# The experts' products as float32 matmuls on four column quarters of TensorE's array, in place of three float32r products on the whole array

## The reference

```python
def moe_swiglu(x, w_router, w_gu, w_down):
    ...
    logits = (t @ w_router).astype(jnp.float32)
    top_v, top_i = lax.top_k(logits, TOP_K)
    top_w = jax.nn.softmax(top_v, axis=-1)
    gates = jnp.sum(jax.nn.one_hot(top_i, N_EXPERTS, dtype=jnp.float32) * top_w[..., None], axis=1)
    out = jnp.zeros_like(t)
    for e in range(N_EXPERTS):
        out = out + gates[:, e:e + 1].astype(t.dtype) * swiglu(t, w_gu[e], w_down[e])
```

## Time and profile before

| | us |
|---|---|
| median of 3 runs | 1658.79 |
| span of the profiled execution, first to last instruction | 1656.5 |
| PE busy | 1611.3 |
| DVE busy | 1291.2 |
| ACT busy | 1001.0 |
| products of the experts (L569, L1123 to L1130), from first to last | 668.9 to 1635.3 |

### The profile page before, as it was taken

The page is one execution under the profiler, slowest core; times in us unless marked ns, Lnnn a source line. Parts: engine busy times, 40 slices in busy tenths (PEclk is TensorE's granted clock), DMA queues, the critical chain, the costliest instruction groups (busy, mean ns, idle before and its releaser), DMA issues.

```text
span 1656.5 us, 30082 instructions
## 1 busy us (share of the span) xinstructions
PE 1611.3 (97%) x12174; PEld 1272.0 (77%) x12174; DVE 1291.2 (78%) x1274; ACT 1001.0 (60%) x1043; POOL 127.5 (8%) x148
## 2 busy tenths in 40 slices
PE   8999999999999998999999999999999999999997
PEld 6779999959889977777776776777777777777775
DVE  4766555487844476898998998998998998998996
ACT  4755443346422235777776777777777777776774
POOL 3330001200035412000000000000000000000000
PEclk9999999999999999999999999999999999999999
DMA  9533546514300012699999999999999999999991
GB/s 258 204 125 127 177 177 230 180 39 143 112 4 4 4 50 88 242 369 374 358 364 374 357 371 371 356 368 374 357 367 372 359 366 372 358 369 371 359 371 52
DMA packets 60916, 425.42 MB, mean 257 GB/s; under 512 B 6999, under 2 KB 8135, under 8 KB 10104
## 3 DMA queue, kind: packets, MB, share of 16 engines
q1 hardware_dynamic: 58776, 416.52, 66.6%
q0 software_dynamic: 2016, 7.13, 1.8%
HBM read 422.28 MB, written 1.12 MB: 256 GB/s over the span
## 4 chain that ended last, share of the span: by engine, by line
PE 74%; DVE 2%; issue 1%; ACT 1%; POOL 0%; ACTq 0%; DVEq 0%
PE PS L569 56%; PE PS L899 6%; PE PS L570 5%; PE PS L1150 1%; PE PS L918 1%; PE PS L1080 1%; PE PS L927 1%; DVE arena L1524 1%; PE PS L625 0%; PE PS L1113 0%; PE PS L1114 0%; PE PS L890 0%; PE PS L1016 0%; PE PS L833 0%; PE PS L883 0%
## 5 line engine op out<-in xcount | busy, mean ns | idle before, releaser
L1524 DVE TENSOR_TENSOR w_lo<-ring,w_hi 128x2048 fp32r<-128x2048 f32 x391 | 896.0, 2293 | 174.0 <-ACT w_hi L1451 86.0
L1451 ACT ACTIVATE w_hi<-ring 128x2048 fp32r<-128x2048 f32 x334 | 641.0, 1919 | 264.2 <-PE PS L569 239.0
L569 PE MATMUL PS<-w_hi,x_hi 128*96 128x512 f32 x896 | 353.8, 395 | 0.7 <-ACT x_hi L1443 0.7
L569 PE MATMUL PS<-w_hi,x_lo 128*96 128x512 f32 x896 | 352.5, 393 | 0.0
L569 PE MATMUL PS<-w_lo,x_hi 128*96 128x512 f32 x896 | 243.0, 392 | 0.0
L1217 ACT ACTIVATE w_hi<-ring 128x2048 fp32r<-128x2048 f32 x55 | 105.3, 1915 | 157.2 <-issue 83.9
L569 PEld LDWEIGHTS PS<-w_lo,x_hi 128*96 128x96 f32 x896 | 144.6, 161 | 62.1
L569 PEld LDWEIGHTS PS<-w_hi,x_lo 128*96 128x96 f32 x896 | 144.8, 162 | 58.4
L569 PEld LDWEIGHTS PS<-w_hi,x_hi 128*96 128x96 f32 x896 | 144.6, 161 | 57.9 <-ACT x_hi L1443 1.0
L569 PE MATMUL PS<-w_hi,hid_hi 128*96 128x512 f32 x444 | 175.1, 394 | 0.0
L569 PE MATMUL PS<-w_hi,hid_lo 128*96 128x512 f32 x444 | 174.5, 393 | 0.0
(11 more groups left out here) (290 smaller groups left out, 2060.5 us busy)
## 6 DMA issues: line engine op xcount, KB each, us to landing
ring<-in_slabs SPq DMA_DIRECT2D x394, 1024.0 KB, 4.8
arena<-in_lora POOLq DMA_DIRECT2D x1, 1152.0 KB, 5.4
h<-in_h SPq DMA_DIRECT2D x2, 544.0 KB, 5.6
arena<-bias_lines POOLq DMA_DIRECT2D x1, 1056.0 KB, 20.9
arena<-bias_lines POOLq DMA_DIRECT2D x1, 1040.0 KB, 26.3
ring<-in_slabs SPq DMA_DIRECT2D x4, 256.0 KB, 8.3
arena<-in_lora POOLq DMA_DIRECT2D x1, 1024.0 KB, 12.3
out<-h SPq DMA_DIRECT2D x4, 256.0 KB, 2.2
```

What stands on the lines that cost most here:

```text
L569: return pe.matmul(out, x, w, start=start, stop=stop) if tokens_stay else \
L1451: act.activation(w_hi[:, n % 2, :], ring[:, n % SLOTS, :], ACT.Copy).then_inc(hi_set, 1)
L1524: tt = lambda o, a, b, op=ALU.mult: dve.tensor_tensor(out=o, in0=a, in1=b, op=op)
```

## The change

The split of the experts' slabs is gone: PE multiplies float32 weights straight from the ring by float32 tokens (`x_all`) or hidden values (`hid_T`). The 96 tokens are three blocks of 32. The array is used as four column quarters. The first three each hold one block and multiply it by a piece of the weights with 384 columns (gate, up), or 512 and then 256 (down). The fourth quarter takes the columns that are left, for one block after another: three matmuls of 128 columns (gate, up) or of 256 (down). A gate/up slab is 4 x (3 + 3) matmuls, a down slab 2 x (3 + 2 + 3 + 1). The results of the fourth quarter lie in PSUM partitions 96 to 127; sigmoid and products run over 128 partitions and 384 columns instead of 96 and 512, and the transposes are three of 128 x 128. Before rounding an expert's output, ACT copies the fourth quarter's part to `y_side` in three pieces. SP waits for `slab_used` (PE's end with a slab) in place of `slab_taken`. `gather` adds high and low parts in one PSUM bank; ACT and DVE keep every second one. `products_by_half` is gone. The passes above the first are changed in the same way and are not run with these inputs.

```diff
+BLK = 32
+BLOCKS = CAP // BLK
+MAIN = BLOCKS * P
+OUT_MAIN, OUT_SIDE = 768, 256
...
-            with sp.Fori(1, N_SLABS // SLOTS) as i:
-                for j in range(SLOTS):
-                    sp.wait_ge(slab_taken, SLOTS * i + (j - SLOTS + 1))
...
+            more_slabs(SLOTS, SL_MOE + SLOTS, slab_taken)
+            more_slabs(SL_MOE + SLOTS, N_SLABS, slab_used)
...
+                def rows_of(j, rows, first):
+                    half, k = divmod(j, KC)
+                    for t in range(TT):
+                        mm = pe.matmul(PS[:, X_BANK[j % 8], 0:HALF], rows[:, t, P * k:P * k + P],
+                                       pick[:, t, 4 * half:4 * half + 4, :].rearrange("p e c -> p (e c)"),
+                                       start=first and t == 0, stop=not first and t == TT - 1)
+                    return mm
...
-                    for j in range(GROUP // P):
-                        mm = pe.transpose(PS[:, 4 + g % 2, CAP * j:CAP * (j + 1)],
-                                          hid_rows[0:CAP, g % 2, P * j:P * (j + 1)], eye[0:CAP, 0:CAP])
+                    for i in range(BLOCKS):
+                        mm = pe.transpose(PS[:, 4 + g % 2, P * i:P * (i + 1)],
+                                          hid_rows[:, g % 2, P * i:P * (i + 1)], eye[:, :])
                     mm.then_inc(hidT_ps, 1)
+                def four(k, bank, col, w, w_main, w_side, width, first, last):
+                    def side(i):
+                        b, c = bank(i), col(i)
+                        return pe.matmul(PS[BLK * BLOCKS:P, b, c:c + width], k(i), w[:, w_side:w_side + width],
+                                         start=first and c == 0, stop=last, skip_group_check=True)
+                    runs = [[i for i in range(BLOCKS) if bank(i) == b] for b in sorted({bank(0), bank(BLOCKS - 1)})]
+                    for run in runs:
+                        b, c, n = bank(run[0]), col(run[0]), width * len(run)
+                        for j in range(BLOCKS):
+                            pe.matmul(PS[BLK * j:BLK * (j + 1), b, c:c + n], k(j),
+                                      w[:, w_main + width * run[0]:w_main + width * run[0] + n],
+                                      start=first, stop=last, skip_group_check=True)
+                        for i in run:
+                            mm = side(i)
+                    return mm
...
+                    pe.wait_ge(loaded[n % SLOTS], 96 * q + 16 * (n // SLOTS + 1))
+                    w = ring[:, n % SLOTS, :]
                     if g < GROUPS:
...
-                        out = PS[0:CAP, 2 * (g % 2) + part // 2, :]
-                        pieces = [(k % 4, x_hi[:, k, at], x_lo[:, k, at], out, k == 0, k == KC - 1)
-                                  for k in range(4 * (part % 2), 4 * (part % 2) + 4)]
+                        for c in range(4):
+                            k = 4 * (part % 2) + c
+                            mm = four(tokens(k), lambda x: 2 * (g % 2) + part // 2, lambda x: P * x, w,
+                                      GROUP * c, GROUP * c + MAIN, P, k == 0, k == KC - 1)
                     else:
...
-                        pe.wait_ge(hid_split, GROUPS * q + ((f + 1) * P // GROUP + 1))
-                        pieces = [(2 * (k - f) + c, hid_hi[:, k, :], hid_lo[:, k, :], PS[0:CAP, 6 + c, :], k == 0, k == FTE - 1)
-                                  for k in (f, f + 1) for c in range(2)]
-                    if e == EXPERTS - 1 and i == SL_EXPERT - 1:
-                        products_by_half(SL_EXPERT * q + (SL_MOE + i), (SL_MOE + i) % 2, pieces)
-                    else:
-                        products(SL_EXPERT * q + (SL_MOE + i), (SL_MOE + i) % 2, GROUP, pieces, tokens_stay=True)
+                        pe.wait_ge(hidT_kept, GROUPS * q + ((f + 1) * P // GROUP + 1))
+                        for c in range(2):
+                            mm = four(hidden(f + c), lambda x: 6 + x // 2, lambda x: OUT_SIDE * (x % 2), w,
+                                      D * c, D * c + OUT_MAIN, OUT_SIDE, f + c == 0, f + c == FTE - 1)
+                    mm.then_inc(slab_used, 1)
...
-            def round_expert_slab(q, i):
...
-                act.activation(w_hi[:, n % 2, :], ring[:, n % SLOTS, :], ACT.Copy).then_inc(hi_set, 1)
...
+            def round_out(q, e):
+                act.wait_ge(slab_used, SL_EXPERT * q + (SL_MOE + SL_EXPERT))
+                for i in range(BLOCKS):
+                    c = OUT_SIDE * (i % 2)
+                    a = act.activation(y_side[BLK * i:BLK * (i + 1), :], PS[CAP:P, 6 + i // 2, c:c + OUT_SIDE], ACT.Copy)
+                a.then_inc(y_moved, 1)
+                gate = slot_gate[0:CAP, e:e + 1]
+                act.activation(yn_hi[0:CAP, 0:GROUP], PS[0:CAP, 6, :], ACT.Copy, scale=gate).then_inc(yn_rounded, 1)
+                act.activation(yn_hi[0:CAP, GROUP:OUT_MAIN], PS[0:CAP, 7, 0:OUT_MAIN - GROUP], ACT.Copy, scale=gate)
+                act.wait_ge(y_moved, q + 1)
+                act.activation(yn_hi[0:CAP, OUT_MAIN:D], y_side[0:CAP, :], ACT.Copy, scale=gate).then_inc(yn_rounded, 1)
...
-            def split_expert_slab(q, i):
...
-                tt(w_lo[:, n % 2, :], ring[:, n % SLOTS, :], w_hi[:, n % 2, :].bitcast(F32), ALU.subtract)\
-                    .then_inc(slab_taken, 1)
...
-                        tt(gue[0:CAP, :], sge[0:CAP, :], PS[0:CAP, 2 * (g % 2), :]).then_inc(gate_used, 1)
+                        if e or g:
+                            dve.wait_ge(rows_set, GROUPS * q + g)
+                        tt(gue, sge, PS[:, 2 * (g % 2), 0:MAIN]).then_inc(gate_used, 1)
```

More of the change, by code:

```diff
@@ L1064, in gather @@
             def gather(o):
-                pe.wait_ge(hn_hi_set, TT * o + TT)
[L1067 to L1078, removed]
-                        for t in range(TT):
-                            mm = pe.matmul(PS[:, 2 * (j % 4) + i, 0:HALF], rows[:, t, P * k:P * k + P],
-                                           pick[:, t, 4 * half:4 * half + 4, :].rearrange("p e c -> p (e c)"),
-                                           start=t == 0, stop=t == TT - 1)
-                        mm.then_inc(done, 1)
+                def rows_of(j, rows, first):
[5 more added lines that the diff above has]
+                    return mm
+                pe.wait_ge(hn_hi_set, TT * o + TT)
+                pe.wait_ge(picked, 2 * o + 1)
+                for j in range(2):
+                    rows_of(j, hn_hi, True)
+                pe.wait_ge(hn_split, TT * o + TT)
+                for j in range(2):
+                    rows_of(j, hn_lo, False).then_inc(x_ps, 1)
+                for j in range(2, JOBS):
+                    if j == KC:
+                        pe.wait_ge(picked, 2 * o + 2)
+                    if j == 6:
+                        pe.wait_ge(rt_dve, RT_FLAG)
+                    if j >= 8:
+                        pe.wait_ge(x_kept_v if j % 2 else x_kept_a, KC * o + (j // 2 - 3))
+                    rows_of(j, hn_hi, True)
+                    rows_of(j, hn_lo, False).then_inc(x_ps, 1)
             def gates_of_slots(o):
@@ L1115, in scatter @@
                 mm.then_inc(scattered, 1)
-            def products_by_half(n, b, pieces):
-                w = lambda x, c: x[:, b, GROUP * c:GROUP * (c + 1)]
-                pe.wait_ge(hi_set, n + 1)
-                for half in range(2):
-                    for c, hi, lo, out, start, stop in pieces[half::2]:
-                        pe.matmul(out, hi, w(w_hi, c), start=start, stop=False)
-                        mm = pe.matmul(out, lo, w(w_hi, c), start=False, stop=False)
-                    if half == 0:
-                        pe.wait_ge(slab_taken, n + 1)
-                    else:
-                        mm.then_inc(hi_free, 1)
-                    for c, hi, lo, out, start, stop in pieces[half::2]:
-                        mm = pe.matmul(out, hi, w(w_lo, c), start=False, stop=stop)
-                    mm.then_inc(slab_used if half else out_half, 1)
             def sums_of_last_norm(added):
@@ L1429, in _ @@
                 act.activation(out_hi[:, k, TEXT], r_[:, k, TEXT], ACT.Copy).then_inc(out_hi_set, 1)
-            for n in range(SL_O2 + 2, SL_MOE + EARLY):
+            for n in range(SL_O2 + 2, SL_MOE):
                 round_slab(n)
@@ L1547, in residual @@
                                                      op0=ALU.mult, op1=ALU.add).then_inc(zsum[l], 1)
-                    if base + n + 2 <= SL_MOE and n < slabs - 1:
+                    if base + n + 2 < SL_MOE and n < slabs - 1:
                         split_slab(base + n + 2)
```

138 lines of the change are left out of this document (61 added, 77 removed).

## The result

The changed kernel takes 1630.1 us (median of 4 runs, 1628.1 to 1634.3) against 1659.4 us in 4 runs of the kernel before taken beside it: ratio 0.982, 95% interval 0.980 to 0.984. It is 29 us faster. The forecast was 1626 us.

What follows compares the result with a forecast made beforehand. TensorE, busy 97% of the span, was taken as the bound. 1656.5 - 57.1 (products) + 22.7 (visits) + 2.1 (tail) = 1624.2 us; with 2.3 from span to median 1626.5, given as 1626, range 1607 to 1666.

Steps and rivals of the forecast that it cites:

- What bounds the kernel: Experts' stage: TensorE, busy 97% of 1656.5 us, ends last; rounding and subtracting leave engines that don't set the end.
- Products: Experts' slabs: float32 products on four quarters take 876.3 us in place of 933.4, a gain of 57.1 us.
- Visits: Transposes and scatters between quarter products: changing to the whole array and back adds 22.7 us, bounds 0 and 45.
- Strict order: Rival on the experts' products: matmuls start and end strictly in program order, near 2735 us; chance 0.01.
- First rival: Chunk edges: a quarter holds too few waiting records, so weight loads are bare; 1664 us, at worst 1720; chance 0.13.
- The ring: Rival on the experts' weight loads: transfers already set the limit, stage keeps 966 us, 1661 us in all; chance 0.07.
- Visits cost double: Rival on the mode changes around transposes and scatters: twice the price, 1649 us; chance 0.07.
- Side work and gather: Hidden values and output copies beside the products cost nothing; gather gains nothing to one microsecond, taken as nothing.
- Tail: After the last product: copies and rounding put the second scatter at 3.6 us, adding 2.1 us, bounds 1 and 4.

Runs made afterwards that it cites:

- experiment 2: Three edits of the changed kernel: transposes done twice, 1647.7 us; two groups' transposes in one visit, 1624.8 us; transposes as identity products on the quarters, 1632.0 us.
- experiment 6: Changed kernel with paired transposes and both scatters of an output in one visit, 1621.7 us; with rounding first, filled tail pause and filled group norm too, 1617.6 us.
- experiment 3: Changed kernel with short pieces issued before long ones in each chunk, 1649.6 us; with all short pieces of a slab after all its long ones, 1924.0 us.
- experiment 1: Changed kernel with half of the experts' products left out and every load kept: 1536.7 us in one run.
- fill_tail: Changed kernel with ten float32 products without use between the last product and the last expert's scatter: 1628.2 us, ratio 0.981 to the kernel before.

## Why the prediction was right, and where it wasn't

- *What bounds the kernel:* right. VectorE and ScalarE lost 1421 us of work, and the span moved by what TensorE saved.
- *Products:* right, under 1 us off. Between visits the starts of the fourth quarter's records make a gate/up slab 2.62 us (forecast 2.616) and a down slab 2.59 (forecast 2.592): 877 us for all of them, forecast 876.3. Four different streams side by side keep the pace that the trace showed for one stream in four. The fourth quarter sets it: its short records come three in 0.33 us, 0.65 a chunk, while the long ones come every 0.32 and run a little ahead (in the changed kernel from 0.02 to 0.10 us between 1188.65 and 1193.89).
- *Visits:* right. 933.1 less 877 leaves 56 us (56 x 0.61, 14 x 1.27 for the scatters, 3.6 for expert 0). Before, 33.0 of 966.4 us weren't products, so 23 are added, forecast 22.7. The mechanism is shown by experiment 2. The fixed part is 0.29 us, and 0.33 by the stage of experiment 6, where the rows of lines 790 and 792 gave 0.33.
- *Strict order:* by the Trainium skill, "TensorE: Matmul & The Clock Gate", Part 3, matmuls start and end in program order. The trace disagrees on the ends: the first short matmul stands behind three long ones in the program, and its two records are over by 1188.82, where the second records of the long ones start at 1188.63 and end at 1189.13. That matmuls on different quarters go side by side is another matter, which the rule doesn't deny; its time of 2735 us came from reading it record by record. That they don't run ahead without limit is what experiment 3 adds.
- *First rival (a quarter holds too few waiting records):* not in this order, where the chain's chunks stay at 0.65 us. The limit exists, at two matmuls; with all short pieces in a row it costs 0.88 us a slab (3.49 against 2.61 in the mean).
- *The ring:* right that it isn't the limit, and the reason (a share of 0.96 isn't full) is borne out by 420 GB/s in experiment 1. Landing went from 4.8 to 7.0 us in the median, inside the lead of 13 us.
- *Visits cost double:* no.
- *Side work and gather:* no wait of TensorE behind them shows in the stage. VectorE has 500 us, forecast 490. The start moved by 0.2 us, within what the clock does there by itself.
- *Tail:* the term that was sized wrong. "Added 2.1 us; bounds 1 and 4": it was 3.9, close to the upper bound. "Second scatter at 3.6 us" holds where the clock does: 3.8 in `fill_tail`. In the changed kernel it is 4.6, since the eight records ahead of it run at 1.2 GHz. So the chain up to there was right, and what was left out is the clock, which fell in this tail, and what lies behind the scatters: with the clock held the tail is still 2.8 us longer, not 2.1, and the unexplained wait ahead of the sums of squares has more than that in it (2.5 us for 1.6). The pause of 2.7 us was in my own sum, but no term for the clock.

Sum as measured: -56.4 for products, +23.1 for visits, +3.9 for the tail, +0.2 for the start, -29.2. The time was 4 us over the forecast: 1.8 for the tail, 0.7 for products, 0.4 for visits, 0.2 for the start, 0.5 that the forecast rounded off its own sum, and the rest from the distance between one execution and the median.

## What to carry to other kernels

When a full engine is relieved, ask first whether it ends last: here 1421 us came off two engines, and all of the gain is that a third does the products in 6% less time (877 us for 933.4). In these runs column quarters work side by side if each finds its next matmul within two of its own; put the shortest pieces last before the array is used whole, and gather such visits, at about 0.3 us each. Where a change lengthens a pause of TensorE in front of work on the critical path, ask for two prices, the pause and the clock behind it: here the clock fell behind a pause of 2.7 us in six profiles of nine, and cost up to 2.7 us.

## What the runs showed of the hardware that was not expected

- A quarter takes two matmuls, one going and one waiting, and not tens ahead (3.49 us a slab with the short pieces in a row, 2.61 in turn).
- Going between quarters and the whole array costs 0.29 us a visit with transposes and 0.33 with scatters, and nothing for products with the identity that stay on the quarters.
- The clock fell within 4.1 us of the last product in six of nine tails with a pause of 2.7 us and held until 11.7 us in three; it fell after a pause of 2.2 us (side pieces on VectorE) and held for over 19 us in both tails with the pause filled. In the group norm it fell with TensorE busy for 4.92 of 5 us, which no run here explains.
- A DMA share of 0.98 at 380 GB/s was not the limit; 1.01 at 420 GB/s was.
